# Splitting one gate unit less in each chunk of the packed experts

## The chip, the core and the metric

The kernel runs on one NeuronCore of a Trainium2 chip. Its engines work side by side and meet through semaphores: TensorE (PE; its weight loads are PEld), VectorE (DVE), ScalarE (ACT), GpSimd (POOL) and SyncE (SP), which here issues the weight loads; 16 DMA engines move the data. The metric is the device time of one execution in microseconds (us), lower is better.

## What is computed

One sequence of 256 tokens with 1024 features passes through two hybrid layers, a pooling layer with a gated network, and a sparse attention layer with a mixture of eight experts, all in float32. The change is in the experts:

```python
def swiglu(x, w_gu, w_down):
    g, u = jnp.split(x @ w_gu, 2, axis=-1)
    return (jax.nn.silu(g) * u) @ w_down

def moe_ffn(x, router, w_gu, w_down):
    ...
    logits = (xt @ router).astype(jnp.float32)
    top_v, top_i = lax.top_k(logits, TOP_K)
    ...
    for e in range(N_EXPERTS):
        y = y + combine[:, e:e + 1] * swiglu(xt, w_gu[e], w_down[e])
```

with TOP_K = 2, N_EXPERTS = 8 and 3584 hidden columns per expert. In the kernel "up" is the half that goes through the silu and "gate" the half that multiplies it.

## The kernel before

**Units.** All weights come as units of 128 partitions x 2048 floats (1 MB). An expert has seven chunks of 512 hidden columns; a chunk has two units of up columns, two of gate columns and two of down rows. The order within an expert is up 0, up 1, gate 0, gate 1 for a chunk and, from chunk 2 on, down 0 and down 1 of the chunk two before; the last two chunks' down units follow at the end: 42 units. A slot index is `u % NSLOT` for a unit number `u`.

**The path of a unit.** SyncE loads it into one of four slots of `ring` (`sync_program`, L2656). TensorE's fast form of float32 (`F32R`) keeps fewer bits, so every unit is split: ScalarE copies it to `HI`, rounded (`split_hi`, L479), VectorE computes `LO` = ring - HI (`split_lo`, L487). HI and LO have three slots each (`NHL`), so the HI split of unit u waits for TensorE's last matmul of unit u-3. That is the semaphore `used`; the end of an LO split is `low`. SyncE waits for `low` of unit u-4 before it loads unit u: from then on nobody reads the ring's slot.

**TensorE.** With a tile of 128 tokens (kind `P`) the tokens are split too, and every product takes three matmuls (`group3`, L497). An expert with at most 64 tokens takes the packed form (kind `PACK`): the high and low parts of its 64 tokens lie side by side in the 128 columns of the left operand, and a product takes two matmuls, with HI and with LO (`group2`, L507). `col_part` does an up or gate unit, `row_part` a down unit. `net_tensor` runs over the chunks: up, gate, then what `mid` holds (in chunk 0 the scatter of the expert before, in chunk 1 the token lists, in chunk 2 the fetch of the next expert's tokens), then the turn of the chunk before (L988 packed, L993 full) and the down rows of the chunk two before.

**ScalarE and VectorE** go through the same chunks in `net_scalar` and `net_vector`. Their splits run AHEAD = 2 units in front of TensorE's place. ScalarE also evicts: L951 the up result, L959 the gate result of a packed chunk, L1003 the silu of the turned chunk, L1019 the packed hidden columns. In a packed chunk its order is split, split, L951, split, split, L959, L1003, split, L1019, split. All these queues are in order.

**Which form runs** is decided at run time. Experts are sorted by their number of tokens, descending, and `two_sides` writes both forms of an expert behind a branch; `KINDS` lists them. Experts 3 to 6 are either (P,) or (PACK,), expert 7 is always (PACK,), and expert 0 may have tiles of both kinds. SyncE's program has no branch.

Of the kernel before, what the change touches and what calls it, by code (L numbers as in the profile page):

```python
# [9 lines left out]
F32 = mybir.dt.float32  # L10
# [6 lines left out]
P = 128  # L17
# [152 lines left out]
class Lane:  # L170


    def __init__(self, e, signals=()):
        self.e, self.signals, self.seen, self.u = e, signals, {}, 0
        self.dma_start = e.dma_start
        for s in signals:
            s.restart()
# [186 lines left out]
def build(nc, d, out, tables):  # L364
    at, cons_cols, units, place = tables
    dense = len(units) - N_EXP * d["experts"].shape[1]
    with ExitStack() as ctx:
# [100 lines left out]
        def hi_lo(u):  # L468
            k, n = units[u]
            h = (u % NHL) * UNIT  # L470
            return [t[:, h:h + k * n].rearrange("p (k n) -> p k n", k=k) for t in (HI, LO)]

        def split_hi(e, n=1):
            for u in range(e.u, min(e.u + n, len(units))):
                m = units[u][0] * units[u][1]
                r, h = (u % NSLOT) * UNIT, (u % NHL) * UNIT
                e.wait_ge(s_ring[u % NSLOT], 16 * (u // NSLOT + 1))
                e.wait_ge(*used.of(u - NHL))
                e.activation(HI[:, h:h + m], ring[:, r:r + m], ACT.Copy).then_inc(*high.up(u))  # L479
            e.u += n  # L480

        def split_lo(e, n=1):
            for u in range(e.u, min(e.u + n, len(units))):
                m = units[u][0] * units[u][1]
                r, h = (u % NSLOT) * UNIT, (u % NHL) * UNIT
                e.wait_ge(*high.of(u))
                e.tensor_tensor(LO[:, h:h + m], ring[:, r:r + m], HI[:, h:h + m].bitcast(F32),  # L487
                                ALU.subtract).then_inc(*low.up(u))
            e.u += n
# [27 lines left out]
        def col_part(e, use, t, u, i, last, kinds, a, x_ready):  # L517
# [4 lines left out]
            for w in x_ready(t):  # L522
                e.wait_ge(*w)
            e.wait_ge(*low.of(u))
            if kinds[t] == P:
                xh, xl = (XTH, XTL) if u < dense else (XM[:, 0], XM[:, 1])
# [1773 lines left out]
        def expert_tensor(e, x, side):  # L2300
# [13 lines left out]
            if x < LAST:  # L2314
                mid[6 if nt == 2 else 2] = lambda: fetch_tensor(e, x + 1, 0, 1 - hf, side,
                                                                ahead(x + 1))
            net_tensor(e, use, f"moe{x}", MOE_CHUNKS, kinds, True,
                       pair(x) + (pair(x + 1) if nt == 2 else []), x_here, hf, mid=mid)
            if nt == 2:
                scatter_tensor(e, x, 1, pair(x + 1), side)  # L2320
# [38 lines left out]
        def expert_scalar(e, x, side):  # L2359
# [8 lines left out]
            if x < LAST:  # L2368
                mid[6 if nt == 2 else 2] = lambda: fetched_hi(e, ("fetch", x + 1, 0, side), 1 - hf,
                                                           ahead(x + 1))  # L2370
            net_scalar(e, use, f"moe{x}", MOE_CHUNKS, kinds, True, mid=mid)
            if nt == 2:
                split_hi(e)
                scatter_scalar(e, x, 1, pair(x + 1), side)
# [135 lines left out]
        def expert_vector(e, x, side):  # L2510
# [20 lines left out]
            if x < LAST:  # L2531
                mid[6 if nt == 2 else 2] = lambda: fetched_lo(e, ("fetch", x + 1, 0, side), 1 - hf,
                                                           ahead(x + 1))
            else:
                mid[2] = residue
            net_vector(e, use, f"moe{x}", MOE_CHUNKS, kinds, True, mid=mid)
            if nt == 2:
                split_lo(e)
                scatter_vector(e, x, 1, side)
# [98 lines left out]
        def sync_program(e):  # L2638
# [4 lines left out]
            for u, (k, n) in enumerate(units):  # L2643
# [4 lines left out]
                else:  # L2648
# [5 lines left out]
                    src = d["experts"][bass.ds(which[x], 1), i].rearrange("o p m -> (o p) m")  # L2654
                e.wait_ge(*low.of(u - NSLOT))
                e.dma_start(ring[:, r:r + m], src).then_inc(s_ring[u % NSLOT], 16)  # L2656
# [64 lines left out]
```

## Time and profile before

| | |
|---|---|
| median of 3 runs | 2424.33 us (2420.62 to 2428.99) |
| profiled execution | 2426.37 us |
| span in its profile | 2424.6 us |
| TensorE matmuls busy | 2160.1 us (89%) |
| VectorE busy | 1602.9 us (66%) |
| ScalarE busy | 1327.3 us (55%) |
| LO splits (L487) | 491 instructions, 1108.1 us |
| HI splits (L479) | 491 instructions, 927.4 us |

The experts are the last 1000 us or so of the span. The busy shares are means over stages with different limits, so the rows below are taken by stretch. Matmuls overlap: a record's duration is longer than the distance to the next one.

### The profile page before, as it was taken

The page shows a single profiled execution, that of the slowest core. Times are in us where ns is not written, and L with a number is a line of the kernel's source. Part 1 is how long each engine was busy: PE and PEld are TensorE (multiplying, and loading weights), DVE is VectorE, ACT ScalarE, POOL GpSimd, SP SyncE. Part 2 cuts the span into 40 slices and gives each one's busy share as a digit, 9 for nine tenths or more (in the row PEclk, how much of TensorE's full clock was granted, in tenths as well). Part 3 has the DMA queues.
Part 4 walks back from the last instruction along what each step waited for, and adds up shares of the span by engine and source line. Part 5 has one row for each costly group of instructions (what it writes and reads, how often), then busy time and mean ns, then how long its engine had stood idle before and what let it go on. Part 6 is the DMA issues. An engine that isn't in the chain of part 4 may idle for free.

```text
span 2424.6 us, 25828 instructions
## 1 busy us (share of the span) xinstructions
PE 2160.1 (89%) x9918; PEld 1740.7 (72%) x9918; DVE 1602.9 (66%) x1539; ACT 1327.3 (55%) x1374; POOL 22.2 (1%) x33
## 2 busy tenths in 40 slices
PE   6888999888999899888768999999999888888886
PEld 5667887766887688676657887887888666666664
DVE  3865554775555544665644555888888788888887
ACT  4554443544443344445524444676767677777775
POOL 0000000000000000000000000000000000000000
PEclk9889999989999999996978999999999999999999
DMA  6314553422655355341015555798989899999995
GB/s 244 132 45 143 181 190 117 171 81 103 224 186 181 106 191 189 126 141 36 1 49 212 208 209 182 300 357 316 369 319 375 303 348 344 354 342 346 360 351 223
DMA packets 74357, 524.54 MB, mean 216 GB/s; under 512 B 8704, under 2 KB 9152, under 8 KB 11872
## 3 DMA queue, kind: packets, MB, share of 16 engines
q1 hardware_dynamic: 71424, 511.64, 56.7%
q0 software_dynamic: 2784, 10.93, 1.3%
q8 instruction: 92, 1.51, 0.2%
q14 instruction: 57, 0.47, 0.1%
HBM read 521.48 MB, written 1.05 MB: 216 GB/s over the span
## 4 chain that ended last, share of the span: by engine, by line
PE 65%; DVE 14%; ACT 9%; DMA 8%; issue 5%; SPq 0%; DVEq 0%; ACTq 0%
PE psum L497 48%; DMA ring<-in_experts 7%; PE psum L507 6%; DVE LO L487 5%; ACT HI L479 5%; PE psum L2265 1%; PE psum L779 1%; PE psum L988 1%; PE psum L993 1%; PE psum L842 1%; DVE AR L1462 1%; PE psum L2293 1%; PE psum L1822 1%; DVE XT L670 1%; PE psum L655 1%
## 5 line engine op out<-in xcount | busy, mean ns | idle before, releaser
L487 DVE TENSOR_TENSOR LO<-ring,HI 128x2048 fp32r<-128x2048 f32 x491 | 1108.1, 2266 | 531.4 <-ACT HI L479 527.1
L479 ACT ACTIVATE HI<-ring 128x2048 fp32r<-128x2048 f32 x491 | 927.4, 1893 | 464.9 <-PE psum L497 284.3
L497 PE MATMUL psum<-HI,XT 128*128 128x512 f32 (+1 forms) x2592 | 841.9, 400 | 54.3 <-DVE XT L670 30.2
L497 PEld LDWEIGHTS psum<-HI,XT 128*128 128x128 f32 x2592 | 503.2, 195 | 174.5 <-DVE XT L670 34.2
L497 PE MATMUL psum<-LO,XT 128*128 128x512 f32 (+1 forms) x1296 | 514.2, 397 | 0.0
L507 PE MATMUL psum<-HI,XT 128*128 128x512 f32 x560 | 236.2, 422 | 67.7 <-DVE LO L487 64.9
L497 PEld LDWEIGHTS psum<-LO,XT 128*128 128x128 f32 x1296 | 253.0, 195 | 50.1
L507 PE MATMUL psum<-LO,XT 128*128 128x512 f32 x560 | 226.5, 404 | 1.1 <-issue 1.1
L497 PE MATMUL psum<-HI,HTH 128*128 128x512 f32 x568 | 225.2, 396 | 0.1
L497 PE MATMUL psum<-HI,HTL 128*128 128x512 f32 x568 | 221.6, 390 | 0.0
L497 PE MATMUL psum<-LO,HTH 128*128 128x512 f32 x568 | 221.2, 389 | 0.0
L507 PEld LDWEIGHTS psum<-HI,XT 128*128 128x128 f32 x560 | 109.5, 195 | 124.5 <-issue 62.7
L507 PEld LDWEIGHTS psum<-LO,XT 128*128 128x128 f32 x560 | 109.6, 196 | 23.8 <-issue 2.5
L507 PE MATMUL psum<-HI,HTH 128*128 128x512 f32 x280 | 114.2, 408 | 11.6 <-DVE HTH L1045 6.3
L497 PEld LDWEIGHTS psum<-HI,HTL 128*128 128x128 f32 x568 | 106.6, 188 | 22.7
L497 PEld LDWEIGHTS psum<-HI,HTH 128*128 128x128 f32 x568 | 106.7, 188 | 21.4 <-issue 0.7
L951 ACT ACTIVATE AR<-psum 128x512 f32<-128x512 f32 (+1 forms) x107 | 63.3, 591 | 107.1 <-PE psum L497 92.5
L497 PEld LDWEIGHTS psum<-LO,HTH 128*128 128x128 f32 x568 | 106.8, 188 | 21.0
L507 PE MATMUL psum<-LO,HTH 128*128 128x512 f32 x280 | 110.5, 395 | 0.0
L507 PEld LDWEIGHTS psum<-HI,HTH 128*128 128x128 f32 x280 | 53.1, 190 | 29.1 <-DVE HTH L1045 8.0
L1009 ACT ACTIVATE HTH<-psum 128x512 fp32r<-128x512 f32 (+1 forms) x72 | 42.7, 594 | 55.5 <-PE psum L993 51.0
L662 ACT ACTIVATE XT<-psum 128x512 fp32r<-128x512 f32 x40 | 23.9, 597 | 88.2 <-PE psum L655 86.7
(269 smaller groups left out, 1774.3 us busy)
## 6 DMA issues: line engine op xcount, KB each, us to landing
ring<-in_experts SPq DMA_DIRECT2D x336, 1024.0 KB, 6.1
ring<-in_dense SPq DMA_DIRECT2D x149, 1024.0 KB, 4.8
bcs<-in_ln_g POOLq DMA_DIRECT2D x4, 512.0 KB, 4.5
bcs<-in_ln_b POOLq DMA_DIRECT2D x4, 512.0 KB, 5.1
bcs<-in_norm_g POOLq DMA_DIRECT2D x3, 512.0 KB, 3.7
cons<-in_cons POOLq DMA_DIRECT2D x1, 1317.0 KB, 8.1
X<-in_x SPq DMA_DIRECT2D x2, 512.0 KB, 4.0
AR<-in_poolm POOLq DMA_DIRECT2D x1, 1024.0 KB, 6.9
```

What stands on the lines that cost most here:

```text
L479: e.activation(HI[:, h:h + m], ring[:, r:r + m], ACT.Copy).then_inc(*high.up(u))
L487: e.tensor_tensor(LO[:, h:h + m], ring[:, r:r + m], HI[:, h:h + m].bitcast(F32), ALU.subtract).then_inc(*low.up(u))
L497: ins = e.matmul(out_ap, lhsT=a, rhs=b, start=start and n == 0, stop=stop and n == m - 1)
L507: ins = e.matmul(out_ap, lhsT=both, rhs=b, start=start and n == 0, stop=stop and n == m - 1)
L655: ins = e.transpose(bank[:, j * P:(j + 1) * P], src(k0 + j), ident)
L670: e.tensor_tensor(XTL[:, k0:k0 + 4, tile(t)], banks.get(name, "cols", t, k0).rearrange("p (k s) -> p k s", k=4), XTH[:, k0:k0 + 4, tile(t) ...
L779: e.matmul(bank[:, 0:2 * nk], lhsT=a.qT[:, b, tile(qt)], rhs=a.kz(kind, b)[:, :, 0:nk], start=True, stop=True).then_inc(*filled.up(a.name, ...
L842: ins = e.matmul(bank[:, col:col + 64], lhsT=a.PT2[:, n % 2, tile(h * kt + i)], rhs=a.v(kind, i, head), start=i == 0, stop=i == kt - 1)
L951: e.activation(GS[:, hb, t, 0:n], banks.get(use, "up", c, t)[:, 0:n], f).then_inc(*a_bank.up(use, "up", c, t))
L988: ins = e.matmul(bank[:, o:o + PACK], lhsT=src[:, tile(j)], rhs=C("pairs"), start=True, stop=True)
L993: ins = e.transpose(bank[:, tile(j)], GS[:, hb, t, tile(j)], ident)
L1009: e.activation(HTH[:, hb, 0:nb, tile(t)], bank[:, 0:n].rearrange("p (j s) -> p j s", j=nb), ACT.Copy).then_inc(*a_done.up(use, "turn", c, t))
```

## The change

Of every chunk of every expert the second gate unit is put in a set, `WHOLE`. While TensorE, ScalarE and VectorE run an expert whose only kind is PACK (`e.packed`), ScalarE and VectorE pass such a unit over, and TensorE multiplies it straight from the ring in float32: four matmuls instead of eight, behind a wait for the load itself. The next unit's split raises its semaphore by two, so that the counts stay. SyncE now waits for TensorE's last use of a `WHOLE` unit before it loads the slot again, in place of the LO split. It does so for all experts, those with full tiles included.

```diff
--- before.py
+++ after.py
@@ -172,6 +172,7 @@
 
     def __init__(self, e, signals=()):
         self.e, self.signals, self.seen, self.u = e, signals, {}, 0
+        self.packed = False
         self.dma_start = e.dma_start
         for s in signals:
             s.restart()
@@ -470,22 +471,33 @@
             h = (u % NHL) * UNIT
             return [t[:, h:h + k * n].rearrange("p (k n) -> p k n", k=k) for t in (HI, LO)]
 
+
+
+        WHOLE = {place[(f"moe{x}", "gate", c, 1)] for x in range(N_EXP) for c in range(7)}
+
         def split_hi(e, n=1):
             for u in range(e.u, min(e.u + n, len(units))):
+                if e.packed and u in WHOLE:
+                    continue
                 m = units[u][0] * units[u][1]
                 r, h = (u % NSLOT) * UNIT, (u % NHL) * UNIT
                 e.wait_ge(s_ring[u % NSLOT], 16 * (u // NSLOT + 1))
                 e.wait_ge(*used.of(u - NHL))
-                e.activation(HI[:, h:h + m], ring[:, r:r + m], ACT.Copy).then_inc(*high.up(u))
+                skipped = 1 if e.packed and u - 1 in WHOLE else 0
+                e.activation(HI[:, h:h + m], ring[:, r:r + m], ACT.Copy).then_inc(
+                    *high.up(u, by=1 + skipped))
             e.u += n
 
         def split_lo(e, n=1):
             for u in range(e.u, min(e.u + n, len(units))):
+                if e.packed and u in WHOLE:
+                    continue
                 m = units[u][0] * units[u][1]
                 r, h = (u % NSLOT) * UNIT, (u % NHL) * UNIT
                 e.wait_ge(*high.of(u))
+                skipped = 1 if e.packed and u - 1 in WHOLE else 0
                 e.tensor_tensor(LO[:, h:h + m], ring[:, r:r + m], HI[:, h:h + m].bitcast(F32),
-                                ALU.subtract).then_inc(*low.up(u))
+                                ALU.subtract).then_inc(*low.up(u, by=1 + skipped))
             e.u += n
 
 
@@ -521,8 +533,17 @@
             bank = banks.get(*use, t)
             for w in x_ready(t):
                 e.wait_ge(*w)
-            e.wait_ge(*low.of(u))
-            if kinds[t] == P:
+            whole = e.packed and u in WHOLE
+            if whole:
+                e.wait_ge(s_ring[u % NSLOT], 16 * (u // NSLOT + 1))
+            else:
+                e.wait_ge(*low.of(u))
+            if whole:
+                w = ring[:, (u % NSLOT) * UNIT:(u % NSLOT + 1) * UNIT].rearrange("p (k n) -> p k n", k=kk)
+                for k in range(kk):
+                    ins = e.matmul(bank[:, 0:n], lhsT=XP[:, i * kk + k, 2 * a:2 * a + P].bitcast(F32),
+                                   rhs=w[:, k, :], start=i + k == 0, stop=last and k == kk - 1)
+            elif kinds[t] == P:
                 xh, xl = (XTH, XTL) if u < dense else (XM[:, 0], XM[:, 1])
                 ins = group3(e, bank[:, 0:n], [
                     (xh[:, i * kk + k, a:a + P], xl[:, i * kk + k, a:a + P], hv[:, k, :], lv[:, k, :])
@@ -2314,8 +2335,10 @@
             if x < LAST:
                 mid[6 if nt == 2 else 2] = lambda: fetch_tensor(e, x + 1, 0, 1 - hf, side,
                                                                 ahead(x + 1))
+            e.packed = kinds == (PACK,)
             net_tensor(e, use, f"moe{x}", MOE_CHUNKS, kinds, True,
                        pair(x) + (pair(x + 1) if nt == 2 else []), x_here, hf, mid=mid)
+            e.packed = False
             if nt == 2:
                 scatter_tensor(e, x, 1, pair(x + 1), side)
 
@@ -2368,7 +2391,9 @@
             if x < LAST:
                 mid[6 if nt == 2 else 2] = lambda: fetched_hi(e, ("fetch", x + 1, 0, side), 1 - hf,
                                                            ahead(x + 1))
+            e.packed = kinds == (PACK,)
             net_scalar(e, use, f"moe{x}", MOE_CHUNKS, kinds, True, mid=mid)
+            e.packed = False
             if nt == 2:
                 split_hi(e)
                 scatter_scalar(e, x, 1, pair(x + 1), side)
@@ -2533,7 +2558,9 @@
                                                            ahead(x + 1))
             else:
                 mid[2] = residue
+            e.packed = kinds == (PACK,)
             net_vector(e, use, f"moe{x}", MOE_CHUNKS, kinds, True, mid=mid)
+            e.packed = False
             if nt == 2:
                 split_lo(e)
                 scatter_vector(e, x, 1, side)
@@ -2652,7 +2679,7 @@
                         which = [e.e.value_load(order[0:1, r:r + 1], min_val=0, max_val=N_EXP - 1)
                                  for r in range(N_EXP)]
                     src = d["experts"][bass.ds(which[x], 1), i].rearrange("o p m -> (o p) m")
-                e.wait_ge(*low.of(u - NSLOT))
+                e.wait_ge(*(used if u - NSLOT in WHOLE else low).of(u - NSLOT))
                 e.dma_start(ring[:, r:r + m], src).then_inc(s_ring[u % NSLOT], 16)
             for t in range(2):
                 e.wait_ge(*v_done.of("l3", "rows", t))
```

TensorE, in the last chunk of expert 7, from the second half of gate unit 0 to the turn; before:

```order
L507 MATMUL psum<-LO,XT 128x512
L507 MATMUL psum<-HI,XT 128x512 [waits s_low]
L507 MATMUL psum<-LO,XT 128x512
L507 MATMUL psum<-HI,XT 128x512
L507 MATMUL psum<-LO,XT 128x512
L507 MATMUL psum<-HI,XT 128x512
L507 MATMUL psum<-LO,XT 128x512
L507 MATMUL psum<-HI,XT 128x512
L507 MATMUL psum<-LO,XT 128x512
L988 MATMUL psum<-cons,AR 128x64 [waits s_a_bank]
```

and after:

```order
L519 MATMUL psum<-HI,XT 128x512
L519 MATMUL psum<-LO,XT 128x512
L544 MATMUL psum<-ring,XT 128x512 [waits s_ring2]
L544 MATMUL psum<-ring,XT 128x512 x3
L1009 MATMUL psum<-cons,AR 128x64 [waits s_a_bank]
```

The eight matmuls on HI and LO have become four on the ring, and the wait for `s_low` one for the load.

ScalarE, in a late chunk of expert 7, where `s_ring0` to `s_ring3` name the slots; before:

```order
L479 ACTIVATE HI<-ring 128x2048 [waits s_used,s_ring1]
L479 ACTIVATE HI<-ring 128x2048 [waits s_used,s_ring2]
L951 ACTIVATE AR<-psum 128x512 [waits s_a_done,s_used]
L479 ACTIVATE HI<-ring 128x2048 [waits s_ring3]
L479 ACTIVATE HI<-ring 128x2048 [waits s_used,s_ring0]
L959 ACTIVATE AR<-psum 128x512 [waits s_a_bank,s_used]
L1003 ACTIVATE AR<-psum 128x256 [waits s_a_bank,s_filled]
```

and after:

```order
L487 ACTIVATE HI<-ring 128x2048 [waits s_used,s_ring1]
L972 ACTIVATE AR<-psum 128x512 [waits s_a_done,s_used]
L487 ACTIVATE HI<-ring 128x2048 [waits s_ring3]
L487 ACTIVATE HI<-ring 128x2048 [waits s_used,s_ring0]
L980 ACTIVATE AR<-psum 128x512 [waits s_a_bank,s_used]
L1024 ACTIVATE AR<-psum 128x256 [waits s_a_bank,s_filled]
```

The split of the slot 2 unit, which is gate unit 1, is gone; all others stand where they stood, among them the split behind L1003.

SyncE's queue, near its end; before:

```order
L2656 ISA [waits s_low]
L2656 DMA ring<-in_experts 128x2048
L2656 ISA [waits s_low]
L2656 DMA ring<-in_experts 128x2048
```

and after:

```order
L2683 DMA ring<-in_experts 128x2048
L2683 ISA [waits s_used]
L2683 DMA ring<-in_experts 128x2048
L2683 ISA [waits s_low]
L2683 DMA ring<-in_experts 128x2048
```

One load in each chunk waits for `s_used`; those behind it in the queue wait with it.

## Rows read from the trace of the kernel before

**Rows 1.** Busy time by stretch: us, PE, PEld, DVE, ACT, POOL, PEclk, DMA share, GB/s.
```profile
1767.00:1900.00 133.00, 129.69 (x585) 106.07 (x583) 113.65 (x68) 92.45 (x63) 0.00 (x0) 1.00 0.90 349
...
1893.00:2410.00 517.00, 431.79 (x1951) 325.80 (x1950) 421.00 (x265) 372.99 (x300) 0.00 (x0) 0.97 0.89 337
...
2041.00:2058.00 17.00, 14.75 (x64) 10.53 (x65) 16.02 (x15) 11.52 (x13) 0.00 (x0) 1.00 0.76 283
...
2107.00:2124.00 17.00, 13.45 (x63) 9.77 (x61) 14.05 (x8) 12.85 (x11) 0.00 (x0) 1.00 0.96 359
```

**Rows 2.** The lines L1003 and L2356, whole span: ns min/median/max, first and last start.
```profile
L1003 ACT ACTIVATE AR<-psum x35: 384/385/388, 1330.4 to 2396.7; 128x256 f32<-128x256 f32 x35
...
L2356 ACT ACTIVATE AR<-psum x18: 574/597/598, 1504.8 to 2407.5; 128x512 f32<-128x512 f32 x18
```

**Rows 3.** Waits from 1640 to 1893 us: us in total, times, longest.
```profile
ACT HI L479 <- PE psum L497: 36.7, 48, 4.2
...
ACT HI L479 <- DMA ring<-in_experts: 1.0, 1, 1.0
```

**Rows 4.** Waits from 1893 to 2405 us.
```profile
ACT HI L479 <- DMA ring<-in_experts: 58.5, 72, 2.7
...
ACT HI L479 <- PE psum L507: 35.3, 19, 6.9
```

**Rows 5.** DMA from 2085 to 2160 us: packets, MB, share; issues, KB, us to landing.
```profile
q1 hardware_dynamic: 3828, 27.84, 97.7%
...
ring<-in_experts SPq DMA_DIRECT2D x27, 1024.0 KB, 7.0
```

**Rows 6.** DMA issues from 1767 to 1900 us, median us to landing last.
```profile
ring<-in_experts SPq DMA_DIRECT2D x44, 1024.0 KB, 5.1
```

**Rows 7.** DMA issues from 2074 to 2081.3 us.
```profile
ring<-in_experts SPq DMA_DIRECT2D x2, 1024.0 KB, 4.8
```

**Rows 8.** Chain of waits from 1839 to 1873 us, expert 3: start, us, what.
```profile
1845.60 16.70 PE psum L497 x72
1862.30 0.44 PE psum L993 x4
```

**Rows 9.** Chain of waits from 2041 to 2092 us, expert 5, chunks 1 and 2.
```profile
2050.60 2.09 PE psum L507 x8
...
2052.71 2.13 PE psum L507 x8
...
2055.06 1.75 PE psum L988 x16
...
2064.51 2.12 PE psum L507 x8
```

**Rows 10.** Chain of waits from 2085 to 2130 us, expert 5, chunks 4 and 5.
```profile
2093.90 1.93 ACT HI L479
...
2095.84 2.30 DVE LO L487
...
2098.30 6.96 DMA ring<-in_experts
```

**Rows 11.** f32 matmuls: timeline of expert 5's chunk 0, then line L2293 whole.
```profile
2041.80 3.70 PE L2293 MATMUL psum<-AR 128*128 128x512 f32 x8 [1.12 <-ACT AR L2356]
...
L2293 PE MATMUL psum<-AR x64: 590/592/697, 1505.5 to 2299.1; 128*128 128x512 f32 x64
```

**Rows 12.** Timeline of ScalarE, expert 5, chunks 5 and 6: start, us.
```profile
2107.78 1.91 ACT L479 ACTIVATE HI<-ring 128x2048 fp32r<-128x2048 f32 x1 [0.27 <-DMA ring<-in_experts]
2110.24 1.92 ACT L479 ACTIVATE HI<-ring 128x2048 fp32r<-128x2048 f32 x1 [0.55 <-DMA ring<-in_experts]
2112.70 1.91 ACT L479 ACTIVATE HI<-ring 128x2048 fp32r<-128x2048 f32 x1 [0.54 <-DMA ring<-in_experts]
...
2141.88 1.92 ACT L479 ACTIVATE HI<-ring 128x2048 fp32r<-128x2048 f32 x1 [0.23 <-DMA ring<-in_experts]
```

**Rows 13.** Timeline of VectorE and ScalarE, expert 3, chunk 5.
```profile
1855.94 2.29 DVE L487 TENSOR_TENSOR LO<-ring,HI 128x2048 fp32r<-128x2048 f32 x1 [0.51 <-ACT HI L479]
...
1865.59 1.92 ACT L479 ACTIVATE HI<-ring 128x2048 fp32r<-128x2048 f32 x1 [0.40 <-PE psum L497]
```

## The prediction

> **What bounds the kernel now.** The table of stretches first, because the change touches only the expert stage. It shows three regimes [rows 1]. Expert 3, at 1767 to 1900 us, runs with a full tile of 128 tokens: TensorE is busy 129.69 of 133 us. Experts 4 to 7, at 1893 to 2410 us, take the packed form (at most 64 tokens): there TensorE is busy 431.79 of 517 us and VectorE 421.00, and neither is full. Inside a packed expert the start differs from the rest: at 2041 to 2058 us VectorE is busy 16.02 of 17 us with the DMA share at 0.76, at 2107 to 2124 us VectorE has 14.05 and the DMA share is 0.96. The counts of two rows say which experts are packed: 35 silu evictions of L1003 are five experts of seven chunks, of which expert 0 is the mixed one (128 + 64); 18 evictions of L2356 are nine tiles of two, so one expert has two tiles and seven have one [rows 2]. So four experts, with 28 chunks, are (PACK,) alone.
>
> Then the waits. With full tiles ScalarE's split waits 48 times for TensorE (36.7 us) and once for a DMA (1.0 us) [rows 3]. In the packed experts it is turned round: 58.5 us for DMAs, 35.3 for TensorE [rows 4]. The queue confirms it: from 2085 to 2160 us its packets fill 97.7% of the 16 engines and a unit lands 7.0 us after its issue [rows 5]; in expert 3 that is 5.1 us [rows 6]; where the queue had run dry it is 4.8 us [rows 7].
>
> Last the chain of waits. In expert 3 it is TensorE without a break: 16.70 + 0.44 us per chunk [rows 8]. In a packed expert's chunks 1 and 2 it runs through TensorE: gate unit 0 (2.09), gate unit 1 (2.13 and 2.12), then the 16 small matmuls of the turn (1.75), and only behind them the eviction and ScalarE's next split [rows 9]. In later chunks it is the ring: DMA 6.96, split HI 1.93, split LO 2.30, the next issue [rows 10].
>
> **What the change does, part by part.**
>
> *Taken away.* 28 HI splits and 28 LO splits. They pay only where VectorE or ScalarE is what the end waits for; gate unit 0 and the units behind gate unit 1 keep both splits.
>
> *Longer on TensorE.* Gate unit 1 was 8 matmuls in 2.12 us. It becomes 4 matmuls of f32. The trace has them at L2293: every one is two records (64 for the 32 of the eight scattered tiles), and eight records, four matmuls, take 3.70 us, with the last one's 0.59 us tail in it [rows 11]. I take 3.5. So the unit costs 1.4 us more. Nothing comes off on the same engine: TensorE reaches it when unit 0 is through, and by then it has long landed.
>
> Where this lies on the chain: chunks 1 and 2 of each packed expert [rows 9]. ScalarE's program puts L959, L1003 and then the next split behind this very unit and its turn, so 1.4 us passes on whole. In chunk 0 the unit is followed by scatters that wait for ScalarE, which covers it; in chunk 3 the chain goes over the unit before. 4 experts x 2 x 1.4 = **+11 us** (ends: 0 if something else came last anyway, +17 if chunk 3 pays too).
>
> *Later release of a ring slot, packed experts.* Before, the slot of gate unit 1 came free at its LO split. Take chunk 5: the splits of its two gate units start at 2110.24 and 2112.70 [rows 12], so unit 1's LO ended 1.93 + 2.30 us later, at about 2116.95. Now it comes free with the last f32 matmul: unit 0's LO ends at 2114.5, its matmuls 2.2 us later (2.09 and the wait), unit 1's 3.5 us after that, 2120.2. That is 3.3 us late. The cover is the queue's depth: a landing of 7.0 us where 4.8 would do [rows 5, 7], 2.2 us. What is over, 1.1 us per chunk, is the upper end; the lower is 0. The issue behind it on SP's queue (for the next down unit) waits at most 0.3 us, and ScalarE's split and TensorE wait behind the landing. For the value I close the loop: issue 0.16 (an LO split ends at 2098.14, the load starts at 2098.30 [rows 10]), landing 4.8 to 5.1, the next landing 2.46 behind (2110.24 to 2112.70), HI and LO 4.24, unit 0's matmuls 2.2, the f32 unit 3.5: 17.4 to 17.7 us per chunk. Measured are 34.10 us for two chunks, 17.05 each (2107.78 to 2141.88) [rows 12]. I take +0.5 for four steps (chunks 3, 4, 5, 6) of four experts: **+8 us** (0 to +18). These units' freed splits win nothing here, because the queue is at 97.7%.
>
> The Trainium skill ("DMA: Bandwidth & Descriptors", Anatomy of one DMA) gives about 2.0 us + bytes / 436 GB/s, an estimate of 4.4 us for such a unit; the trace's shortest median is 4.8 [rows 7]. By the page both loops would be 0.4 us shorter and the two ring terms together some 11 us smaller.
>
> *Later release, full tiles.* SP's program is the same for all experts, so experts 1 to 3, which still split everything, wait for TensorE's last use too. In chunk 5 of expert 3 the LO split of gate unit 1 ends at 1858.23 and its matmuls at 1862.30 [rows 8, 13]: 4.1 us late. The split four units on starts at 1865.59; with 4.8 us it could have landed at 1863.2, so 2.4 us are covered and 1.7 are not: the upper end. HI slots come free by TensorE, so LO is a little ahead of it, and part of the 1.7 is covered there. The loop says how much: issue 0.16, landing 5.1, HI and LO 4.25, three units of 16.70 / 6 = 2.78 us: 17.9 against 17.14 [rows 6, 8]. I take +0.7 for four steps (chunks 3 to 6; at chunks 0 to 2 the fetch and scatter give more cover) of three experts: **+8.4 us** (0 to +20). Expert 0, with two tiles and twice the TensorE time, has cover enough.
>
> **Sum.** 11 + 8 + 8.4 = +27 us. The profiled execution took 2426.4 us, 1.8 of it outside the span, and is 2 us over the median of 2424.3; against the median: 2452 us. All ends together: 2424 to 2479.
>
> **Rivals.**
>
> *VectorE's relief counts (faster).* At 2041 to 2058 us VectorE is 94% busy [rows 1]; if it is the bound of chunks 1 to 3, each saves an LO split of 2.30 us: 4 x 3 x 2.3 = -28, with +8 from the full tiles -20: 2404 us. It decides if the split behind gate unit 1 starts earlier. Against it: on the chain the LO split stands before gate unit 0, and the next split waits for HI buffers and L1003, both TensorE's [rows 9]. Chance 0.12. The Trainium skill ("Perfetto Trace Analysis", Identifying the Most-Contended Engine) ranks VectorE by occupancy and TensorE by weight loads, which puts VectorE first here; taken at its word, 28 LO splits would be -64 us. The trace disagrees in the last chunks, where neither is full and the queue is.
>
> *All is covered (no change).* The jitter of landings already leaves TensorE waiting, and the longer unit and the late release fall into those waits. For it: 4.8 to 7.0 us landings and 83% TensorE share. Against: the two chunks where TensorE is on the chain, and expert 3, where it never waits. About 2427 us. Chance 0.10.
>
> *The late release bites whole.* Each uncovered part counts in full: 17 + 18 + 20 = +55: 2479 us. It decides if the queue runs dry once in every chunk, in all seven experts. For it: 2.2 and 2.4 us of cover are little beside 3.3 and 4.1 us of lateness. Chance 0.08.
>
> *The change does less than it says.* If the flag were not set in the taken branch, no f32 matmul would run and only the release would move: +16. It lies in the range; the order of the changed program shows the f32 rows.
>
> **Chances.** Forecast 0.70, with its own range 2436 to 2470. Faster rival 0.12, no change 0.10, whole release 0.08. To leave out no more than 2 in 10 the range goes from 2426 to 2480: it leaves out the faster rival and some of the edges. A measurement of this kernel tells about 0.3%, 7 us, from no change. Faster by more than that 0.12, within 0.10, slower 0.78.
>
> **What will show it.** Right: 28 x 4 f32 matmuls of 3.4 to 3.7 us per unit; LO and HI splits 463 each; L1003 in chunks 1 and 2 of a packed expert some 1.4 and 2.8 us later against its start; experts 1 to 3 longer by 2 to 4 us each, with ScalarE's split waiting for DMAs where it waited once; SP waiting for TensorE; the queue's share in 97.7% chunks lower. Wrong: experts 1 to 3 with unchanged length (the full tiles' term falls), packed experts shorter than 126 us with VectorE's share down (the first rival), or a DMA share of the later chunks as high as before with longer chunks, which would mean slower packets and not a dry queue.

## The result and the profile after

The changed kernel takes **2463.16 us** (median of 4 runs, 2458.61 to 2465.72), the kernel before 2424.93 us on the same chip (4 runs, 2420.62 to 2428.99): ratio 1.0148, 95% interval 1.0130 to 1.0167, or +36 us (the two medians are 38 us apart; the ratio is the one on record, and the differences below go by such ratios). It is slower, as forecast (2452), and inside the range, but by 36 us where the sum had 27. The profiled execution took 2458.61 us, its span is 2455.7 us.

The changed code stands 12 to 27 lines further down: HI split L487, LO split L499, group3 L509, group2 L519, the f32 matmuls L544, the gate units' turn L1009 (packed) and L1014 (full tile), SP's load L2683. The page of the changed kernel, engines first, then groups (busy us, mean ns | idle before):

```profile
PE 2195.5 (89%) x9918; PEld 1735.1 (71%) x9918; DVE 1542.7 (63%) x1511; ACT 1278.3 (52%) x1346; POOL 22.2 (1%) x33
...
L499 DVE TENSOR_TENSOR LO<-ring,HI 128x2048 fp32r<-128x2048 f32 x463 | 1046.6, 2265 | 614.3 <-ACT HI L487 608.0
L487 ACT ACTIVATE HI<-ring 128x2048 fp32r<-128x2048 f32 x463 | 874.4, 1891 | 475.6 <-PE psum L509 261.5
...
L544 PE MATMUL psum<-ring,XT 128*128 128x512 f32 x224 | 100.6, 592 | 0.0
```

463 splits of each kind (28 fewer) and 224 records of f32 matmul, two for each of 4 x 28: the change does what it says. The same stretches as [rows 1] after the change: us, PE, PEld, DVE, ACT, POOL, PEclk, DMA share, GB/s.

```profile
1767.00:1900.00 133.00, 130.15 (x576) 103.93 (x576) 109.77 (x66) 90.70 (x63) 0.00 (x0) 1.00 0.86 333
1893.00:2410.00 517.00, 450.26 (x1901) 316.09 (x1900) 353.60 (x231) 317.52 (x264) 0.00 (x0) 0.98 0.85 333
```

In the packed experts VectorE fell from 421.00 to 353.60 us and TensorE rose from 431.79 to 450.26. The granted clock is 0.98 in place of 0.97, so TensorE stood less at the lower of its two levels (1.2 GHz, full is 2.4); more of that below. Relief and price are both there; only the price shows in the time. The DMA share fell in both stretches, so packets did not fill the queue better: loads start later.

Waits of the changed kernel, from 1640 to 1893 us (experts 2 and 3; ScalarE, then SP's queue up to 1900 us), then from 1893 to 2405 us:

```profile
ACT HI L487 <- DMA ring<-in_experts: 43.0, 41, 2.2
...
ACT HI L487 <- PE psum L509: 16.2, 12, 4.2
```
```profile
SPq L2683 <- PE psum L509: 82.7, 14, 6.6
```
```profile
ACT HI L487 <- DMA ring<-in_experts: 74.6, 85, 2.3
```

Against one wait for a DMA and 48 for TensorE [rows 3], ScalarE's split in experts 2 and 3 now waits 41 times for a DMA and 12 times for TensorE. Expert 3 in the chain of waits of the changed kernel (start, us, what):

```profile
1822.60 16.68 PE psum L509 x72
1839.29 0.04 SPq L2683
...
1839.43 4.78 DMA ring<-in_experts
...
1844.23 1.92 ACT HI L487
...
1846.18 2.30 DVE LO L499
...
1848.53 8.68 PE psum L509 x36
1857.23 0.04 SPq L2683
...
1857.37 4.84 DMA ring<-in_experts
```

Where TensorE ran without a break [rows 8], the chain now goes from its last matmul with gate unit 1 back to SP, through the load and both splits to TensorE again. From 1839.29 to 1857.23 are 17.94 us, the 17.9 that the prediction's loop gave. What it had not is the load *behind* the late one, which goes out 0.5 us later, shares the queue with it and lands later. In expert 2 the chain goes through that load, and the step takes 18.43 us (1724.04 to 1742.47):

```profile
1724.18 0.33 SPq L2683
...
1724.70 7.50 DMA ring<-in_experts
...
1732.22 1.93 ACT HI L487
...
1734.17 2.30 DVE LO L499
...
1736.60 5.86 PE psum L509 x24
```

The late load itself is issued at 1724.18; the line at 1724.70 is the one behind it. From 1767 to 1900 us the median landing is now 6.9 us, at a lower DMA share (5.1 before [rows 6]):

```profile
q1 hardware_dynamic: 6068, 44.16, 85.4%
...
ring<-in_experts SPq DMA_DIRECT2D x43, 1024.0 KB, 6.9
```

Expert 5 in the chain of the changed kernel: chunks 1 and 2, then one whole late chunk.

```profile
2072.13 2.06 PE psum L519 x8
2074.19 3.43 PE psum L544 x8
...
2077.84 1.75 PE psum L1009 x16
...
2085.18 2.08 PE psum L519 x8
2087.26 3.43 PE psum L544 x8
2090.70 3.57 PE psum L2286 x32
2094.27 1.75 PE psum L1009 x16
```
```profile
2122.74 2.08 PE psum L519 x8
2124.83 3.45 PE psum L544 x8
...
2128.43 0.33 SPq L2683
...
2128.95 6.78 DMA ring<-in_experts
...
2135.75 1.93 ACT HI L487
...
2137.70 2.30 DVE LO L499
...
2140.14 2.06 PE psum L519 x8
```

From chunk 1's first gate unit to chunk 2's turn are 22.14 us, before 19.60 (2050.60 to 2070.20; the turn at 2070.20 follows the 3.57 us behind the unit of [rows 9]): two f32 units of 3.43 for 2.12. In the late chunk the ring and TensorE are now one loop: unit 0, the f32 unit, SP's two issues, the load behind, HI, LO, unit 0: 2122.74 to 2140.14, 17.40 us a chunk where it was 17.05 [rows 12].

Per expert: the time between TensorE's last use of an expert's last unit and the next expert's, less that of the kernel before, from one profile of each kernel (us; a single value moves by 2 or 3 us from profile to profile, so only sums and steady signs are used).

```
expert                       0     1     2     3     4     5     6     7
changed kernel             0.0   4.9   5.2   5.3   5.1   7.0   1.4   3.4
release alone              0.0   5.4  11.5   4.9   3.4   5.5   1.7   4.1
release alone, experts 3-7 0.1  -1.1  -0.5   5.3   6.0   1.5  -1.2   6.1
change in chunks 0-2 only  0.2   0.1  -0.8   1.3   4.7   4.4   0.2   4.1
change in chunks 3-6 only  0.0   3.9   7.2   4.6   1.6   5.0   1.4  -0.2
change in experts 3-7      0.0  -1.1  -1.0   4.3   9.3   4.4   1.3   4.6
half of each f32 unit      0.0   4.3   7.3   6.1   9.3   1.1   0.3   1.1
both gate units late       0.0   4.0   5.3   4.5   7.3   1.9   2.9   1.1
before + fifth slot        0.1  -1.1  -1.4   0.0  -3.7  -0.8  -7.1  -9.2
release + fifth slot       0.0  -1.1   3.3   0.0  -0.3   1.1  -8.5  -4.1
change + fifth slot        0.0  -1.1   2.0   0.0   3.5   5.5   0.0  -4.0
up unit 0 + fifth slot     0.1  -1.0  -1.5   0.0   2.7  -2.2  -5.7  -6.8
```

The 11.5 of the release alone holds a stretch at the lower clock: from 1700 to 1735 us its granted clock is 0.90, where the kernel before has 1.00 from 1640 to 1893 us.

### The profile page after: what moved, and what is told of

The parts are those of the page before. It is cut to its first block, busy times and chain, and to the rows that moved or that the text cites. A ratio compares the mean times of both kernels' runs of the same rounds, so it can differ in the third digit from the quotient of the medians.

```text
span 2455.7 us, 25800 instructions
## 1 busy us (share of the span) xinstructions
PE 2195.5 (89%) x9918; PEld 1735.1 (71%) x9918; DVE 1542.7 (63%) x1511; ACT 1278.3 (52%) x1346; POOL 22.2 (1%) x33
## 4 chain that ended last, share of the span: by engine, by line
PE 62%; DVE 14%; DMA 11%; ACT 8%; issue 4%; SPq 0%; DVEq 0%; ACTq 0%
PE psum L509 43%; DMA ring<-in_experts 11%; DVE LO L499 6%; PE psum L519 6%; ACT HI L487 5%; PE psum L544 3%; PE psum L2286 1%; PE psum L800 1%; PE psum L863 1%; PE psum L1009 1%; DVE AR L1483 1%; PE psum L1014 1%; PE psum L1843 1%; DVE XT L691 1%; PE psum L676 1%
## 5 line engine op out<-in xcount | busy, mean ns | idle before, releaser
L499 DVE TENSOR_TENSOR LO<-ring,HI 128x2048 fp32r<-128x2048 f32 x463 | 1046.6, 2265 | 614.3 <-ACT HI L487 608.0
L487 ACT ACTIVATE HI<-ring 128x2048 fp32r<-128x2048 f32 x463 | 874.4, 1891 | 475.6 <-PE psum L509 261.5
L509 PE MATMUL psum<-HI,XT 128*128 128x512 f32 (+1 forms) x2592 | 844.8, 400 | 63.0 <-DVE XT L691 30.2
L509 PEld LDWEIGHTS psum<-HI,XT 128*128 128x128 f32 x2592 | 502.5, 195 | 189.6 <-DVE XT L691 34.2
L509 PE MATMUL psum<-LO,XT 128*128 128x512 f32 (+1 forms) x1296 | 513.6, 396 | 0.0
L509 PEld LDWEIGHTS psum<-LO,XT 128*128 128x128 f32 x1296 | 252.9, 195 | 49.1
L519 PE MATMUL psum<-HI,XT 128*128 128x512 f32 x448 | 187.5, 418 | 61.5 <-DVE LO L499 51.1
L509 PE MATMUL psum<-HI,HTH 128*128 128x512 f32 x568 | 225.9, 398 | 0.7 <-DVE LO L499 0.6
L509 PE MATMUL psum<-HI,HTL 128*128 128x512 f32 x568 | 221.6, 390 | 0.0
L509 PE MATMUL psum<-LO,HTH 128*128 128x512 f32 x568 | 221.3, 390 | 0.0
L519 PE MATMUL psum<-LO,XT 128*128 128x512 f32 x448 | 179.6, 401 | 2.3 <-issue 2.3
L519 PEld LDWEIGHTS psum<-HI,XT 128*128 128x128 f32 x448 | 87.0, 194 | 104.4 <-issue 65.0
L509 PEld LDWEIGHTS psum<-HI,HTH 128*128 128x128 f32 x568 | 106.7, 188 | 24.3 <-DVE LO L499 2.5
L509 PEld LDWEIGHTS psum<-HI,HTL 128*128 128x128 f32 x568 | 106.6, 188 | 22.8
L509 PEld LDWEIGHTS psum<-LO,HTH 128*128 128x128 f32 x568 | 106.8, 188 | 20.8
L519 PE MATMUL psum<-HI,HTH 128*128 128x512 f32 x280 | 113.5, 405 | 6.6 <-DVE HTH L1066 4.3
L519 PE MATMUL psum<-LO,HTH 128*128 128x512 f32 x280 | 109.6, 391 | 0.0
L519 PEld LDWEIGHTS psum<-LO,XT 128*128 128x128 f32 x448 | 87.1, 194 | 20.3 <-issue 3.6
L544 PE MATMUL psum<-ring,XT 128*128 128x512 f32 x224 | 100.6, 592 | 0.0
L1009 PEld LDWEIGHTS psum<-cons,AR 128*128 128x128 f32 x560 | 66.9, 192 | 9.7 <-issue 8.1
L544 PEld LDWEIGHTS psum<-ring,XT 128*128 128x128 f32 x224 | 42.4, 189 | 42.5 <-issue 40.2
```

What stands on the lines that cost most here:

```text
L509: ins = e.matmul(out_ap, lhsT=a, rhs=b, start=start and n == 0, stop=stop and n == m - 1)
L519: ins = e.matmul(out_ap, lhsT=both, rhs=b, start=start and n == 0, stop=stop and n == m - 1)
L544: ins = e.matmul(bank[:, 0:n], lhsT=XP[:, i * kk + k, 2 * a:2 * a + P].bitcast(F32), rhs=w[:, k, :], start=i + k == 0, stop=last and k == ...
L1009: ins = e.matmul(bank[:, o:o + PACK], lhsT=src[:, tile(j)], rhs=C("pairs"), start=True, stop=True)
```

## The experiments

Every kernel ran beside the kernel before on its chip; ratios are against that, with 95% intervals. All are the changed kernel but for the edits shown.

**1. The late release alone, and the change in part of the experts.** The flag off leaves SP's wait and takes the f32 matmuls away:

```
-            e.packed = kinds == (PACK,)      (TensorE, ScalarE, VectorE)
+            e.packed = False
```

> All units are split and multiplied as before; only the release of the ring slot of each chunk's gate unit 1 waits for TensorE's last use, in all experts. Theory (the late release closes a loop issue, landing, splits, TensorE in the experts with full tiles, and an f32 unit lies on the chain in the packed ones): experts 1 to 3 lose what they lost in the changed kernel, +16 us, the packed ones 0 to +3 us, since there the release is 2.2 us late and 2.2 us are covered; about 2442 us. Rival (each f32 unit costs its 1.3 us in full, 28 x 1.3 = 37 us, and the release costs nothing): 2425 us.

Measured 2459.51 us (before 2429.11), ratio 1.0121 (1.0100 to 1.0142): +29 us. The rival that a late release is covered falls. The theory's number was missed too: it had the full tiles' part and next to nothing in the packed experts, but these lose as well. Of the change's 36 us, some 29 come without one f32 matmul. The other cut leaves experts 0 to 2 as before:

```
-        WHOLE = {place[(f"moe{x}", "gate", c, 1)] for x in range(N_EXP) for c in range(7)}
+        WHOLE = {place[(f"moe{x}", "gate", c, 1)] for x in range(3, N_EXP) for c in range(7)}
```

> The changed kernel, with the set of unsplit units cut to experts 3 to 7, so that experts 0 to 2 release their slots at the LO split again. Theory: experts 1 and 2 get their 4.5 and 6.4 us back, 11 us less than the changed kernel, about 2451 us. Rival (f32 units in full): no change against the changed kernel, 2462 us.

Measured 2448.57 us, ratio 1.0088 (1.0067 to 1.0109), as expected. Both edits together, on another chip:

> No unit unsplit; the release of gate unit 1 waits for TensorE in experts 3 to 7 only. Theory: experts 1 and 2 as before, expert 3 +5 us, the four packed ones as in the run with the release alone, +14 us: 18 us over before, 2447 us, within 3 us of the same set with f32 (2448.6 us), so that f32 itself is nearly free once the release is late. Rival (the f32 units' length costs its 1.3 us each): 2429 + 5 = 2434 us.

Measured 2443.44 us (before 2428.93), ratio 1.0066 (1.0047 to 1.0086). The four corners (change, release alone; all experts, 3 to 7) give the terms as differences of ratios: late release in experts 1 and 2, 0.0060 with f32 elsewhere and 0.0055 without, 13 to 15 us; f32 on top of the release, 0.0027 and 0.0022, 5 to 7 us; the rest, 0.0066, 16 us, is the release in expert 3 and the packed experts. Each difference carries some 7 us of uncertainty (95%), the mean of two pairs some 5; the two pairs agree within 1.2. So the release in experts 1 and 2 is clear of noise, the f32 on top of it barely.

**2. Is the f32 unit's length the cause?** Half of it is left out: the unit is multiplied with two of its four row blocks, so half of its product is missing.

```
-                for k in range(kk):
+                for k in range(kk // 2):
```

> The changed kernel, but the f32 unit does only the first two of its four blocks of rows (half of the unit's product is left out): 1.7 us instead of 3.4, less than the 2.1 us of the split form. The slot still comes free only after it. Theory now (the late release is most of the loss, the f32 unit's length a chain term at the start of an expert): experts 1 to 3 keep their 16 us, the packed experts lose the chain term (1.3 us in chunks 1 and 2) and most of the late release, some 0 to +10 us over before: 2445 to 2455 us. Rival (length is what costs, in the packed experts too): packed experts at or under before, 2440 us or less.

Measured 2452.46 us (before 2428.93), ratio 1.0093 (1.0072 to 1.0113). From its chain of waits:

```profile
2157.30 2.08 PE psum L519 x8
2159.39 1.73 PE psum L544 x4
```

A unit of 1.73 us is shorter than the 2.12 of the split one, and the kernel is still 23 us slower than before. Most of that, 17.7 us, lies in experts 1 to 3, which have no f32 unit; the packed experts are 11.9 us longer, and their clock is lower too (0.95 from 1893 to 2405 us, 0.97 before), so how much of the 11.9 is the release is not shown. A faster f32 matmul would not have saved the change.

**3. Both gate units released late, without f32.**

```
-        WHOLE = {place[(f"moe{x}", "gate", c, 1)] for x in range(N_EXP) for c in range(7)}
+        WHOLE = {place[(f"moe{x}", "gate", c, i)] for x in range(N_EXP) for c in range(7)
+                 for i in range(2)}
```

> No unit unsplit; both gate units of every chunk are released by TensorE's last use, which doubles the suspected cost. Theory (a loop is closed once per chunk, and a second late release one unit earlier runs beside the first): +5 to +15 us over the release of one, 2462 to 2475 us. Rival (each late release costs by itself): twice the 29 us, 2487 us.

Measured 2455.39 us (before 2428.93), ratio 1.0119 (1.0099 to 1.0139): the same as one unit late (1.0121) and under what was expected. A price per late unit, which would have doubled it, falls. What costs, as far as these runs tell, is one closed loop through the ring in each chunk; a second late slot beside the first adds nothing that shows.

**4. A fifth ring slot.** If the loop goes through the ring, a deeper ring must open it. The expert units get a fifth 1 MB slot, in AR, columns 12288 to 14335, which nothing else uses in this stage; slots are given round in fives, each with its own semaphore, and SP waits for the unit that held the slot last:

```
+        for u in range(len(units)):
+            s = u % NSLOT if u < dense else (u - dense) % (NSLOT + 1)
+            PREV.append(max((v for v in range(u) if SLOT[v] == s), default=None))
+            SLOT.append(s)
+            USE.append(1 if PREV[u] is None else USE[PREV[u]] + 1)
...
-                e.wait_ge(*(used if u - NSLOT in WHOLE else low).of(u - NSLOT))
-                e.dma_start(ring[:, r:r + m], src).then_inc(s_ring[u % NSLOT], 16)
+                if PREV[u] is not None:
+                    e.wait_ge(*(used if PREV[u] in WHOLE else low).of(PREV[u]))
+                e.dma_start(slot(u, m), src).then_inc(s_ring[SLOT[u]], 16)
```

The kernel before with this, no part of the change:

> The kernel before with the same fifth slot: the control of the run with five slots. Theory: experts 1 to 3 are bound by TensorE and don't move; in the packed experts' late chunks the queue is at 97.7% and can't give much; their start may gain a little from loads that go out earlier: 0 to -12 us, about 2418 us. Rival (depth is what bounds the packed experts): -25 us or more.

Measured **2400.25 us** (2396.75 to 2403.84; before 2429.11), ratio 0.9878 (0.9860 to 0.9895), -29 us: the rival held, and this beats both kernels. The changed kernel with it:

> The changed kernel with a fifth ring slot for the experts' units, in a part of AR that the expert stage doesn't use. Theory: both loops get one unit more of depth (2.5 us or more against 1.1 and 1.7 us that were not covered), so experts 1 to 3 are as long as before and the packed experts keep only the chain term, 1.3 us in two or three chunks each, 10 to 16 us more than the kernel before with five slots. Rival: 37 us more than the kernel before with five slots.

Measured 2428.61 us, ratio 1.0003 (0.9993 to 1.0013): level with the kernel before and 28 us behind its own base, between the two expectations. And the release alone with it:

> The kernel before with a fifth ring slot for the expert units, and only the late release of the change: the slot of gate unit 1 of each chunk comes free with TensorE's last use of it, but both of its splits stay and it is multiplied in fp32r as before. No f32 matmul runs. Theory (with five slots the late release is covered, and what the changed kernel loses there is the f32 unit's own length): the time of the kernel before with five slots, 2400 us, within 7 us: 2397 to 2407. The five-slot version of the whole change took 2428.6, so all of its 28 us would be the f32 unit, some 1.3 us in each of 28 chunks less what the first ones hide. Rival (the late release costs with five slots too, because the whole ring is one slot shorter for part of each chunk): 2410 to 2425.

Measured 2411.10 us (before 2426.20 on this third chip), ratio 0.9929 (0.9907 to 0.9950). The theory was missed: against the five-slot base (1.0052 as a ratio of ratios) the late release still costs about 12 us, less than half of its 29 with four slots, and the f32 unit costs 18 (1.0003 against 0.9929) where with four slots it cost 7; both figures carry some 7 us of uncertainty. In experts 1 and 3 nothing is left of the release's cost.

The chains tell why. One late chunk of expert 5 in the kernel before with five slots, then in the changed kernel with five:

```profile
2100.52 0.39 ACT AR L1015
2100.91 1.81 ACT HI L491
...
2105.37 4.42 DVE LO L499 x2
...
2109.92 2.08 PE psum L519 x8
...
2112.03 2.12 PE psum L519 x8
2114.15 1.75 PE psum L1000 x16
2115.92 0.39 ACT AR L1015
```
```profile
2108.34 2.06 PE psum L531 x8
2110.39 3.43 PE psum L556 x8
2113.83 1.75 PE psum L1021 x16
```

No DMA is in either. The ring's loop of 17.05 us is gone and what is left is the gate step's own cycle, through both gate units, the turn, eviction and splits: 15.40 us a chunk. In it the f32 unit counts nearly whole: 16.67 us from gate unit 1 to gate unit 1, 1.27 more, where 3.43 less 2.12 is 1.31. The release alone has the shorter cycle without the room for it; its chain in the same stretch goes back to the DMA:

```profile
2106.63 0.33 SPq L2696
...
2107.15 9.50 DMA AR<-in_experts
```

Its queue is as full as before (97.0% from 2085 to 2160 us), a load behind the late one takes 9.50 us, and ScalarE's split waits for loads into `ring` 33 times from 1893 to 2405 us (26.6 us; 6 times and 3.1 us in the five-slot base). With the f32 unit the chunk is 1.3 us longer, the queue has air (89.9%), and no load is on the chain there. Read so, release and f32 cover one another in part, and the price of a single edit depends on which loop is the longer; no run tests this reading by itself.

**5. Early and late chunks apart** (four slots).

```
-        WHOLE = {place[(f"moe{x}", "gate", c, 1)] for x in range(N_EXP) for c in range(7)}
+        WHOLE = {place[(f"moe{x}", "gate", c, 1)] for x in range(N_EXP) for c in range(3)}
```

> The changed kernel with four slots, but the unsplit unit and its late release only in chunks 0 to 2 of each expert; chunks 3 to 6 split everything and release early. Theory (in chunks 1 and 2 of a packed expert TensorE is on the chain, so the f32 unit's 1.3 us come in whole, 4 experts x 2 x 1.3 = 10; the late release closes its loop only where the queue has no lead left, from chunk 3 on): +10 to +16 us over the kernel before, about 2441 on this chip. Rival (the loss is one price per late release wherever it stands, 3/7 of the whole 36 us): +15 or more, with experts 1 to 3 longer too; another rival (all loss sits in the late chunks): within 5 us of the kernel before.

Measured 2438.86 us (10 runs; before 2426.20), ratio 1.0056 (1.0034 to 1.0078), +13 us, all of it in the packed experts: experts 1 to 3 stand at +0.1, -0.8 and +1.3. With range(3, 7) in place of range(3):

> The changed kernel with four slots, but the unsplit unit and its late release only in chunks 3 to 6 of each expert. Theory (the loop through the late release is the loss of these chunks): +20 to +28 us over the kernel before, 2449 to 2457, with experts 1 and 2 some 5 us longer each as in the changed kernel; together with chunks 0 to 2 alone it should add up to the whole change's 36 us. Rival (a late chunk's loss is made up while TensorE has other work at the next expert's start): under +15.

Measured 2451.78 us, ratio 1.0094 (1.0064 to 1.0124), +23 to +26 us, experts 1 to 3 longer by 3.9, 7.2 and 4.6. The two add up to 1.0150, the whole change is 1.0148. So the cost comes in the two places that the prediction named: the early chunks of the packed experts, and the late chunks of all experts with one tile. That it is the f32 length in the first and the late release in the second is not split by these two runs, since both edits stand in each.

**6. A better place, with five slots.** The unsplit unit is up unit 0 of chunks 1 to 6 in experts 3 to 7, away from the gate step's cycle:

```
-        WHOLE = {place[(f"moe{x}", "gate", c, 1)] for x in range(N_EXP) for c in range(7)}
+        WHOLE = {place[(f"moe{x}", "up", c, 0)] for x in range(3, N_EXP) for c in range(1, 7)}
```

> A version that might beat both: five ring slots, and the unsplit unit is up unit 0 of chunks 1 to 6 of the packed experts. With five slots the chunk's chain is L1003, HI split, LO split, L1045, two LO splits, two units of TensorE, turn: 15.4 us. With up unit 0 out of it one LO split of 2.2 us leaves that chain, and its f32 matmuls run while TensorE would wait. TensorE alone needs 5 x 1.85 + 3.43 + 1.75 = 14.4 us, the DMA engines about 6 x 2.6 = 15.6 us at the packets' mean. So the chunk stays within -0.6 to +0.3 us: 2390 to 2405 us, against 2400 us for the kernel before with five slots. Rival (each f32 unit costs 1.3 us wherever it stands): 24 x 1.3 = +31 us, 2431 us.

Measured 2414.16 us (before 2428.93), ratio 0.9939 (0.9919 to 0.9960): 9 us above what was expected, and 14 behind the five-slot base. Its chain:

```profile
2087.40 9.62 DMA ring<-in_experts
...
2103.45 1.73 PE psum L1021 x16
2105.18 3.73 PE psum L531 x16
2108.91 3.45 PE psum L556 x8
...
2112.51 5.74 DMA ring<-in_experts
```

Here the unsplit unit stands behind the turn and two down units, so its slot is held through all three, and the loop through the DMA closes again with five slots. Cheap in its place on TensorE, it is dear in the ring. Neither place tried made the unsplit unit pay.

## Why the prediction was right, and where it was off

**The sign and the two mechanisms: right.** A longer unit on TensorE's part of the chain, and a slot that comes free with TensorE's last use and not with the LO split. Nearly all that was to show did: the counts, 3.43 us a unit (3.5 predicted), experts 1 to 3 longer with ScalarE waiting for DMAs (by 4.9 to 5.3 us each, though, not by 2 to 4), SP waiting for TensorE, a lower DMA share (97.7% [rows 5] to 86.3% from 2085 to 2160 us). L1003 was to be 1.4 and 2.8 us later in chunks 1 and 2; in expert 5 it is 1.25 and 2.54. The sign "waiting for DMAs where it waited once" holds for experts 2 and 3, which [rows 3] cover; in expert 1 ScalarE's split waited 17 times for DMAs before (12.2 us) and 18 times after (21.8 us).

**Longer on TensorE, +11: the size is shown only where nothing else moves.** The early chunks alone cost 13 us, with what their late release adds. On top of an already late release the f32 matmuls add 5 to 7 us in all. The step that was off is the bare sum: in the early chunks the f32 length is paid, in the late ones it stands in the loop that the release has closed, and the two terms share some of their time. Chunk 3 pays as well, which the prediction had in its upper end of 17 alone: from TensorE's last use of gate unit 1 in chunk 2 to that in chunk 3, all four packed experts take 1.26 to 1.28 us longer in the changed kernel, and with the release alone three of the four take what they took before.

Something else gives time back, and neither the prediction nor a run prices it: the clock. From 1893 to 2405 us TensorE stood at 1.2 GHz for 34.1 us in the kernel before, for 44.4 with the release alone, and for 20.5 in the changed kernel (means of 0.97, 0.96 and 0.98). At a mean of 0.69 two split gate units took 5.50 us (release alone, from 2088.98) in place of 4.21. The 24 us less at half speed are worth at most 12 us of matmul, an estimate from these figures, so a part of the f32 unit's price may have come back this way. How much is open.

**Late release, full tiles, +8.4: mis-sized by half.** Experts 1 to 3 became 15.4 us longer (4.9, 5.2, 5.3). The closed loop came out right where it stands alone (17.94 against 17.9), in part by luck: the late load landed in 4.78 us where the sum had 5.1, and TensorE's three units took 8.68 where it had 8.34. The failed step is "landing 5.1" as the only landing: it is that of a queue whose loads are 2.3 to 3.7 us apart [rows 6], and this loop, unlike the one for the packed experts, has no second load behind. The late issue holds back the load behind it on SP's queue, the two then run together, the second lands after 7.50 us in expert 2's chain, and the median landing becomes 6.9 us. And +0.7 in each of four steps is the steady loop alone, while the first steps also pay the lateness: between TensorE's last uses of gate unit 1 in expert 2, chunks 3 to 4, 4 to 5 and 5 to 6 take 18.96, 18.43 and 17.96 us, and from there to the expert's last unit 17.93, where the kernel before has 17.14, 17.10, 17.14 and 17.25. The first step's +1.8 is near the prediction's upper end of 1.7, the last one's +0.7 its value.

**Late release, packed experts, +8: right as a sum, too low for the release alone.** The four packed experts became 16.9 us longer together, against 11 + 8, and the late chunk shown runs at 17.40 us, the lower end of 17.4 to 17.7. Over the twelve steps from chunk 3 to chunk 6 of these experts the mean is 17.54 us, 17.13 before: +0.41, where the sum had +0.5. But the release alone is worth 16 us in experts 3 to 7, expert 3's 5 among them, so 11 in the packed ones, and the f32 matmuls come to less than their 11. "The issue behind it waits at most 0.3 us" was wrong, and named the wrong unit: the load behind is that of the next chunk's gate unit 0, the one that the chain needs next. The LO split that frees its slot ended at 2127.86, and it went out at 2128.95, 1.1 us later.

**"Freed splits win nothing, because the queue is at 97.7%": right result, wrong reason.** The queue was no bound. With a fifth slot and nothing else its share is the same, and it moves 5% more; DMA from 2085 to 2160 us in the kernel before with five slots:

```profile
q1 hardware_dynamic: 4016, 29.23, 96.9%
```

Before, it was 27.84 MB in the same 75 us [rows 5]. The late chunks were bound by the ring's depth: load, HI, LO and issue in a loop of four slots. That is also why the freed splits win nothing: the loop goes on through the unit that isn't split, and now through TensorE.

The Trainium skill ("Perfetto Trace Analysis", Identifying the Most-Contended Engine) says not to rank the DMA by occupancy, as with 16 engines it misleads, but by the bandwidth it reaches. These runs agree: by occupancy the queue was full at 27.84 MB and at 29.23. The sum doesn't rest on it.

The fit that the prediction takes from the Trainium skill ("DMA: Bandwidth & Descriptors", Anatomy of one DMA) is given there for loads that GpSimd issues. The 4.4 us worked out from it are thus no figure for these loads, which SyncE issues and of which the quickest shown above landed after 4.78 us. The sum doesn't rest on that either.

**The rivals.** VectorE's relief fell: its 67 us of work less in the packed experts bought nothing that the time shows. With five slots two LO splits stand on the chain of a late chunk (4.42 us for both), but the changed kernel has the same two there, so the split it saves is not one of them, and the longer unit is on that chain. "All is covered" fell in the first experiment. "The release bites whole" (+55) is too much; the truth lies between it and the forecast.

What stays open: that the 12 us of the late release with five slots come from a full queue is read from its chain and its landings; no run lightened the queue to show it.

## What to carry to other kernels

When a buffer comes free is part of an edit's price: the unsplit unit saved 4.2 us of splitting and held its ring slot for TensorE, and most of the loss came from that, even in experts where no unit was unsplit. Before trading work between engines, close the loop through the ring (issue, landing, splits, use) and try one slot more; here that alone gave 29 us. And a wait on an in-order queue also delays the load behind it, so take the landing of two loads together and not of one.

## What the runs showed of the hardware

- A queue's packets can fill 97% of the 16 engines' time at different rates: 75 x 16 x 0.977 / 3828 gives 0.306 us of engine time for a packet [rows 5], the five-slot kernel 0.290 us (0.969 and 4016). The Trainium skill ("HBM Reference", Specifications (TRN2)) has about 425 GB/s for a core that streams alone; no stretch of 75 us here came to that (372 and 391 GB/s in these two; the most in any run is 408, in the kernel before with five slots, from 2211 us).
- A load of 1 MB on an idle or nearly idle queue lands 4.8 us after its issue, time after time (4.78 and 4.84 above, 4.8 in [rows 7]); issued 0.5 us behind another it takes 6.8 us (median of 52 in the changed kernel), and up to 9.6 in the chains with five slots.
- An f32 matmul of 128x512 takes 0.86 us (3.43 for four), an fp32r one 0.26 (2.08 for eight) (both in a stretch at a granted clock of 1.00, 2.4 GHz); so the unit takes 1.6 times as long in f32, though it needs half as many matmuls.
